# First units, a joint finish and gated linear attention on token partitions, in a two-layer hybrid encoder trunk

## What is computed

```
x += 0.5 * SwiGLU_1(RMSNorm(x))                 # 1024 -> 2816 -> 1024
proj = RMSNorm(x) @ w_in                        # q,k,v | q_g,k_g,v_g,gate,r_g
attn = rmsnorm(windowed attention with sinks and ALiBi)          # 512 wide
o    = gla_chunked(q_g, k_g, v_g, log_a)        # 4 heads x 128, chunks of 64
gla  = rmsnorm(o, per head) * silu(r_g)                          # 512 wide
x += concat(attn, gla) @ w_out
x += 0.5 * SwiGLU_2(RMSNorm(x))
```

## Time and profile before

| | |
|---|---|
| median of 3 runs | 932.29 us (932.19 to 932.37) |
| the profiled execution, its own time | 932.18 us |
| its span, first to last instruction | 930.6 us |
| PE busy | 920.4 us, 99% of the span, 8128 matmuls |
| weight loads of PE busy | 913.3 us, 98% |
| DVE, ACT, POOL busy | 606.8, 454.2, 2.8 us |
| loads | 169.04 MB, 182 GB/s over the span |
| granted PE clock, mean | 0.996 of full speed |

### The profile page before, as it was taken

How to read it: one execution, slowest core, us unless ns; L and a number is a source line. 1 busy time by engine, 2 the same in 40 slices (tenths; PEclk the granted TensorE clock), 3 DMA queues, 4 the chain that set the end, 5 groups by cost and what they waited for, 6 DMA issues and landing times.

```text
span 930.6 us, 19276 instructions
## 1 busy us (share of the span) xinstructions
PE 920.4 (99%) x8128; PEld 913.3 (98%) x8128; DVE 606.8 (65%) x699; ACT 454.2 (49%) x499; POOL 2.8 (0%) x6
## 2 busy tenths in 40 slices
PE   9999999999999999999999999999999999999996
PEld 9999999999999999999999999999999999999996
DVE  7765565687768665555685555567796785565554
ACT  6534434458646433444554344436675644434433
POOL 0000000000000000000000000000000000000001
PEclk9999999999999999999999999999999999999998
DMA  8765665563246665666556555655713675655631
GB/s 291 227 225 182 210 195 183 181 189 120 78 159 217 214 203 180 190 193 204 181 187 213 194 181 183 214 188 141 223 47 92 226 227 184 215 188 182 203 111 46
DMA packets 130996, 169.04 MB, mean 182 GB/s; under 512 B 3344, under 2 KB 116752, under 8 KB 130960
## 3 DMA queue, kind: packets, MB, share of 16 engines
q1 hardware_dynamic: 130384, 167.86, 56.5%
q10 hardware_dynamic: 576, 0.66, 0.2%
HBM read 167.46 MB, written 1.05 MB: 181 GB/s over the span
## 4 chain that ended last, share of the span: by engine, by line
PE 96%; DVE 1%; DMA 1%; issue 0%; ACT 0%; SPq 0%; POOLq 0%; DVEq 0%
PE ps L376 30%; PE ps L378 30%; PE ps L377 30%; PE ps L587 1%; PE ps L600 1%; DMA raw<-in_ffn_w_gate 1%; PE ps L437 0%; PE ps L724 0%; DVE wlo L1094 0%; PE ps L747 0%; PE ps L734 0%; SPq L260 0%; PE ps L429 0%; PE ps L794 0%; PE ps L682 0%
## 5 line engine op out<-in xcount | busy, mean ns | idle before, releaser
L1078 DVE TENSOR_TENSOR wlo<-raw,whi 128x2048 fp32r<-128x2048 f32 (+2 forms) x158 | 353.6, 2238 | 238.3 <-ACT whi L820 238.3
L376 PE MATMUL ps<-xhi,whi 128*128 128x256 f32 x1648 | 457.7, 278 | 0.0
L378 PE MATMUL ps<-xhi,wlo 128*128 128x256 f32 x1648 | 455.4, 276 | 0.0
L377 PE MATMUL ps<-xlo,whi 128*128 128x256 f32 x1648 | 455.4, 276 | 0.0
L820 ACT ACTIVATE whi<-raw 128x2048 fp32r<-128x2048 f32 (+2 forms) x158 | 295.8, 1873 | 146.4 <-PE ps L378 146.1
L376 PEld LDWEIGHTS ps<-xhi,whi 128*128 128x128 f32 x1648 | 309.5, 188 | 1.7 <-issue 1.0
L378 PEld LDWEIGHTS ps<-xhi,wlo 128*128 128x128 f32 x1648 | 309.6, 188 | 0.0
L377 PEld LDWEIGHTS ps<-xlo,whi 128*128 128x128 f32 x1648 | 309.5, 188 | 0.0
L376 PE MATMUL ps<-h_parts,whi 128*128 128x256 f32 x768 | 212.4, 277 | 0.9 <-DVE h_parts L1201 0.9
L377 PE MATMUL ps<-h_parts,whi 128*128 128x256 f32 x768 | 212.1, 276 | 0.0
L378 PE MATMUL ps<-h_parts,wlo 128*128 128x256 f32 x768 | 212.1, 276 | 0.0
(11 more groups left out here) (163 smaller groups left out, 498.2 us busy)
## 6 DMA issues: line engine op xcount, KB each, us to landing
raw<-in_ffn_w_down SPq DMA_DIRECT2D x44, 1024.0 KB, 4.9
raw<-in_ffn_w_gate SPq DMA_DIRECT2D x42, 1024.0 KB, 5.4
raw<-in_ffn_w_up SPq DMA_DIRECT2D x42, 1024.0 KB, 5.3
raw<-in_w_in SPq DMA_DIRECT2D x12, 1024.0 KB, 5.1
raw<-in_w_in SPq DMA_DIRECT2D x8, 512.0 KB, 4.6
raw<-in_w_out SPq DMA_DIRECT2D x8, 512.0 KB, 4.5
raw<-in_w_in SPq DMA_DIRECT2D x2, 1088.0 KB, 5.5
raw<-in_w_out SPq DMA_DIRECT2D x8, 256.0 KB, 3.7
```

What stands on the lines that cost most here:

```text
L376: pe.matmul(o, w_hi, x_hi, start=start, stop=False, skip_group_check=True)
L377: pe.matmul(o, w_hi, x_lo, start=False, stop=False, skip_group_check=True)
L378: return pe.matmul(o, w_lo, x_hi, start=False, stop=stop, skip_group_check=True)
L1078: nc.vector.tensor_tensor(lo, r, h.bitcast(F32), ALU.subtract).then_inc(lo_done, 1)
```

## The change

Five edits. (1) In the first units, `square_sums(0)` and `spread_r` move into the fifth piece, DVE's and ACT's pieces of the fourth unit move ahead and wait for less, and the low part of the first down unit is made in two halves. (2) The GLA products and both gate projections are computed with tokens on partitions; the sums of squares come from ACT's accumulator (`osum`), the gate is made by ACT directly from PSUM, norm and gate are applied by DVE in eight products of 128x128, and 8 transposes bring the result back; `gla_sums` and `o32` go. (3) ACT's table for Silu is called up after the attention's squares, not before the blocks. (4) The last two down units are finished together. (5) At the end fewer column sums, other places for the sums' additions, ten transposes that nobody reads (`KEEP`), and another order of two stores. Cut:

```diff
+            def finish_two(turn, grp):
+                def add(m, slot, ft, stop=False):
+                    w_hi, w_lo = weights(slot, ft, D, m * P, P)
+                    return three(sum_of(m, True), w_hi, w_lo, hhi[slot - 1][:, ft, :], hlo[slot - 1][:, ft, :], False, stop)
+                split_ready(1, turn)
+                for m in range(KT):
+                    add(m, 1, 0)
+                for ms in ((0, 1), (2, 3), (4, 5), (6,), (7,)):
+                    for m in ms:
+                        last = add(m, 1, 1)
+                    if ms[0] == 0:
+                        pe.wait_ge(hlo_done, grp + GROUPS)
+                        split_ready(2, turn)
...
+                    for m in ms:
+                        add(m, 2, 0)
+                        last = add(m, 2, 1, stop=True)
+                    last.then_inc(unit_done if ms[0] == KT - 1 else acc_pair, 1)
...
                     piece_lo(0, p, 2)
+                    if p == LAST:
+                        square_sums(0)
...
                     piece_lo(1, p, 7)
+                    if p == LAST:
+                        pe.wait_ge(s_cst, 16)
+                        spread_r(0, rs_y)
                     piece_lo(2, p, 0)
-                    if p == LAST - 1:
-                        square_sums(0)
-                pe.wait_ge(s_cst, 16)
-                spread_r(0, rs_y)
...
-                project(M_R0, t, tiles(0), attention_sums)
+                project_tokens(M_R0, t, [ps[0][:, 0:UC], ps[0][:, UC:2 * UC]], attention_sums)
...
+                for tt in range(TT):
+                    for h in range(GH):
+                        pe.matmul(o_tile(tt, h), AT[:, 4 * (h % 2) + 2 * (h // 2) + tt, :], vg[:, tt, h * P:(h + 1) * P],
+                                  start=tt == 0 and h < 2, stop=False, skip_group_check=True)
...
+                for c in range(1, NCH):
+                    for h in range(GH):
+                        j, b, r = h // 2, DK * (h % 2), CHUNK * (c % 2)
+                        last = pe.matmul(o_tile(c // 2, h)[r:r + CHUNK, :], qe[b:b + DK, j, c * CHUNK:(c + 1) * CHUNK],
+                                         Sta[b:b + DK, c - 1, j, :], start=False, stop=True, skip_group_check=True)
...
-                project(M_R1, t, tiles(0), gla_sums)
+                pe.wait_ge(sg_done, 4 * l + 2)
+                project_tokens(M_R1, t, [ps[0][:, 0:UC], ps[0][:, UC:2 * UC]])
...                                              # PE, behind M_WO + 1
-                        pe.wait_ge(o_ev, 2 * ev)
-                        spread([ps[1], ps[2]], 5 * l + 3, rs_y, 8).then_inc(rG_ps, 1)
+                        pe.wait_ge(og_done, 2 * ev)
+                        for h in range(GH):
+                            for tt in range(TT):
+                                last = pe.transpose(ps[3 * (h // 2)][:, (h % 2 * TT + tt) * P:(h % 2 * TT + tt + 1) * P],
+                                                    o_tok[:, tt, h * P:(h + 1) * P], ident)
...                                              # PE, end
-            tile_sums(4, first=True)
-            tile_sums(5)
-            tile_sums(6)
-            pe.wait_ge(sqsum_done, 3 * DEPTH + 2)
+            tile_sums(6, first=True)
+            pe.wait_ge(sqsum_done, 3 * DEPTH + 1)
             column_sums(sqsum[:, :])
             tile_sums(7, last=True).then_inc(ss_done, 1)
+            for _ in range(KEEP):
+                pe.transpose(ps[1][:, 0:P], ident, ident)
...                                              # ACT, mix
+                def gate_out(i):
+                    act.wait_ge(unit_done, ST + 3 * t + i + 1)
+                    c = UC * (i == M_R1)
+                    for tt in range(TT):
+                        nc.scalar.activation(sg_tok[:, tt, c:c + UC], ps[0][:, tt * UC:(tt + 1) * UC], ACT.Silu,
+                                             scale=rcol[:, tt:tt + 1]).then_inc(sg_done, 1)
+                gate_out(M_R0)
                 split_mix(10)
...
+                for p in range(2):
+                    act.wait_ge(o_ps, 2 * l + p + 1)
+                    for h in (p, p + 2):
+                        for tt in range(TT):
+                            e = nc.scalar.activation(o_sq[:, tt, h * P:(h + 1) * P], o_tile(tt, h), ACT.Square,
+                                                     accum_out=osum[:, GH * tt + h:GH * tt + h + 1])
+                    e.then_inc(osq_done, 1)
+                gate_out(M_R1)
                 split_mix(11)
...                                              # DVE, first block
+                    fourth_lo(0)
+                    norm_r(0, 0, rs_y)
+                    fourth_lo(1)
+                    norm_b(0)
+                    dve.wait_ge(rb_done, 1)
+                    gate_out(0, 0, 2)
+                    fourth_lo(2)
+                    up_out(0, 1, 7)
+                    fourth_lo(3)
+                    half_lo(0)
+                    h_lo(0, 0)
+                    half_lo(1)
...                                              # DVE, mix
+                dve.wait_ge(sg_done, 4 * ev)
+                for tt in range(TT):
+                    for h in range(GH):
+                        c = slice(h * P, (h + 1) * P)
+                        e = nc.vector.scalar_tensor_tensor(out=o_tok[:, tt, c], in0=o_tile(tt, h),
+                                                           scalar=rs_y[:, GH * tt + h:GH * tt + h + 1],
+                                                           in1=sg_tok[:, tt, c], op0=ALU.mult, op1=ALU.mult)
+                    e.then_inc(og_done, 1)
                 split_mix(11)
...                                              # POOL, DVE, end
+            add(flat(2, 4), flat(0, 2), flat(2, 4)).then_inc(pool_sum, 1)
+            pool.wait_ge(pool_sum, 1)
+            add(sqsum[:, :], sq[:, 2, :], sq[:, 3, :]).then_inc(pool_sum, 1)
...
+            last_residual(6, 7, 7)
+            dve.wait_ge(pool_sum, 2)
+            dve.wait_ge(sq_done, 2 * (3 * DEPTH - 1) + 3)
+            add_eps(sqsum[:, :], sqsum[:, :], sq[:, 4, :], D).then_inc(sum_step, 1)
+            dve.wait_ge(sum_step, 7 * (DEPTH - 1) + 9)
+            nc.vector.tensor_tensor(sqsum[:, :], sqsum[:, :], sq[:, 5, :], ALU.add).then_inc(sqsum_done, 1)
+            dve.wait_ge(unit_done, ST + 3 * DEPTH * TURNS)
+            last_residual(7, 8, 2)
```

More of the change, by code:

```diff
@@ L402, in up, with down @@
                 last.then_inc(unit_done, 1)
-            def down(slot, turn, hb, first, alone=False):
-                split_ready(slot, turn)
+            def down(slot, turn, hb, first, alone=False, halves=False):
+                if halves:
+                    pe.wait_ge(half_split, 1)
+                else:
+                    split_ready(slot, turn)
                 for ft in range(FT):
+                    if halves and ft:
+                        split_ready(slot, turn)
                     for m in range(KT):
@@ L544, in ffn @@
                 alone = f == 1 and l == DEPTH - 1
-                down(1, t + 1, 0, True, alone)
-                with pe.Fori(2, GROUPS) as g:
+                down(1, t + 1, 0, True, alone, l == 0 and f == 0)
+                with pe.Fori(2, GROUPS - alone) as g:
                     pe.wait_ge(a_done, grp + g)
@@ L740, in gla_sums @@
-                def gla_sums():
-                    pe.wait_ge(am_done, 4 * l + 2)
-                    for h in (0, 2, 1, 3):
-                        if h < 2:
-                            pe.wait_ge(osq_done, 2 * l + h + 1)
-                        for tt in range(TT):
-                            last = pe.matmul(ps[3][:, 2 * h + tt:2 * h + tt + 1],
-                                             sq[:, 4 + h, tt * P:(tt + 1) * P], ones[:, 0:1],
-                                             start=True, stop=True, skip_group_check=True)
-                    last.then_inc(oss_done, 1)
@@ L864, in ffn @@
                 grp = (2 * l + f) * GROUPS
-                if l or f:
-                    act.wait_ge(table_in, 2 * l + f)
-                    nc.scalar.activation(unread[:, :], ones[:, 0:2], ACT.Silu).then_inc(table_in, 1)
                 if l or f:
@@ L991, in mix @@
-                nc.scalar.activation(sg[:, 2:4, :], sg[:, 2:4, :], ACT.Silu).then_inc(sg_done, 1)
                 split_mix(12)
@@ L994, in mix @@
                 for b in range(2):
[L995 to L996 removed]
+                    act.wait_ge(og_ps, 2 * l + b + 1)
+                    nc.scalar.activation(xhi[:, 4 + 2 * b:6 + 2 * b, :], tiles(3 * b), ACT.Copy,
+                                         scale=par[:, G_GLA:G_GLA + 1]).then_inc(mhi_done, 1)
                 split_mix(14)
```

200 lines of the change are left out of this document (89 added, 111 removed).

## The result

The changed kernel takes 948.24 us (median of six runs, 947.81 to 954.5), the kernel before 932.33 beside it: ratio 1.016, 95% interval 1.0125 to 1.0195. Forecast was 925.6. The change makes the kernel 1.6% slower, though the waits for `sqsum` and `h_parts` that it was made to end are no longer in the list.

The account below looks back on a forecast made before the run. PE was taken to bound the kernel nearly throughout. Head -2.2, two mixers -3.2 and end -1.3 us gave -6.7 us on 932.18, so 925.5, median 925.6 us; range 923.8 to 928.0.

Parts of the forecast that it names:

- a slower pace of the 48-matmul units outside the places touched: Sign of being wrong: units away from the edits slow down; held for unchanged at 5.66 us a unit.
- E: Mixers: chain from M_R1 through second gate, eight products and low part becomes the longest; 934.4 us, chance 0.03.
- the price of the token form: Mixers: token-form units cost +0.19 us for a whole unit, taken as +0.1 each for M_R0 and M_R1.
- Head: First units: PE's early waits shrink and the first down unit starts at 29.5, not 31.75; -2.2 us.
- Mixers: Two mixers: column sums go, -1.7, token form +0.2, output units -0.1; -1.6 us each, -3.2 both.
- The state products: Mixers: 24 products at 55 to 68 ns, 1.3 to 1.6 us, no change; ends -0.45 and +1.1 us.
- Rival B: Mixers: the state products don't overlap, +1.1 us a mixer; 927.8 us, chance 0.10.
- C: Mixers: M_WO + 2 late from costlier products or squares, 0.5 to 1.2 us a mixer; 926.6 to 928.0, chance 0.09.
- End: Kernel's end: column sums -0.4, kept clock -0.5, store order -0.4; together -1.3 us, between -0.3 and -1.7.
- The sums: Kernel's end: 12 sum instructions instead of 20 let DVE go on sooner; -0.4 us, ends 0 and -0.7.
- rival D: Kernel's end: clock falls despite the ten transposes and ACT's order gives nothing; 926.5 us, chance 0.05.

Follow-up runs that it names:

- 12: Kernel before with five stands of PE, behind each mixer's eight spreads and behind the spread of blocks 2 to 4; 937.7 us, ratio 0.986.
- 9: Changed kernel with six stands of PE: ahead of block 1's first down unit, behind each mixer's transposes, behind blocks 2 to 4's spread; 928.2 us, ratio 0.979.
- 6: Changed kernel with a stand of PE behind the eight transposes of each mixer alone; 932.7 us, ratio 0.989.
- 1: Changed kernel with the GLA part, its gate, output norm and Silu table place as in the kernel before; 943.2 us, ratio 1.0025.
- 2: Kernel before with only the GLA part and the Silu table's place changed; 951.0 us, ratio 1.014.
- 17: Changed kernel as it is, run once more on another chip; 951.0 us, ratio 1.012.
- 5: Changed kernel with one stand of PE ahead of the first down unit of each feed-forward block; 929.9 us, ratio 0.989.
- 18: The kernel of 5, run once more on another chip; 930.9 us, ratio 0.992.
- 3: Changed kernel with eight more unread transposes of the old kind behind the eight of each mixer; 956.0 us, ratio 1.018.
- 4: Changed kernel with the 24 state products done a second time, unread, behind each mixer's transposes; 950.1 us, ratio 1.016.
- 13: Changed kernel with the weights of each three products in the order high, low, high; 948.3 us, ratio 1.017.
- 14: The kernel of 5 with its four stands lengthened to 0.65 us by a 192-column memset; 931.4 us, ratio 0.997.
- 11: The kernel of 5 with its four stands lengthened to 0.92 us by a 512-column memset; 951.2 us (recorded ratio covers two of twelve runs).

## Why the prediction was wrong

**The step that failed** is the ground of the sum: "a slower pace of the 48-matmul units outside the places touched, which I hold for unchanged". It changed in three blocks and the output units, +22.3 us, three times what the edit moved. I had read it in the rows, units behind column sums "already run at the slower pace in their second half", and priced it at 0.1 us for a unit. Since the pace holds through a whole block, and a block behind its spread is some 175 us long, the same 4.5 ns an instruction are 6.8 us there. No rival had this mechanism: E, the only slower one, priced a gate chain, and its wait didn't come. The rows also held both paces side by side, and I took them for a property of the form: of the two units in the earlier trace rows, M_KG starts three products in 340 ns and M_V0 in 353 (the trace, 225 and 231 us), and that is the whole of the 0.19 us that I called the price of the token form. M_V0 is slow in both mixers of all 20 traces; M_R1, in the same form, is fast in 17 of its 28 cases. Nor is 0.118 us "the pace of PE": it is 5.66 us over 48 with the gap in it, and the products step by 0.113.

**Head, -2.2 forecast, -1.6 measured.** Both waits go; the sums are at 20.51 (20.25 forecast). The down unit starts at 30.12 for 29.5, and the mis-sized term is the load: ACT waits for the down weights until 24.49, where I had 23.6 (issued 0.5 us later and landed after 5.6 us for 5.2). The chain behind it, to the end of `h_lo` at 30.06, took 5.6 us for 5.7. In the other traces with this head ACT starts on them at 24.0 to 25.3. And 0.2 us of the 1.6 is the pace of the fourth unit, not the edit.

**Mixers, -1.6 each forecast, -2.6 and -2.3 measured** up to the transposes. The state products were mis-sized: 43 ns, the lower bound, 0.47 us under before, where I took no change. The rest is pace: M_R1 ran fast where I added 0.1 us, and in the first mixer so did one unit ahead of the GLA part (0.2 us). Rival B is out, and C too: PE doesn't wait for the low part behind the transposes. The Trainium skill (TensorEngine Tiling (Array Packing), "When to Use Tiling"), which I did not follow, was nearer: it has such tiles gain up to twice the speed from the swap. The trace agrees in part: 1.49 to 1.02 us is a third less, not half.

**End, -1.3 forecast, -0.4 measured.** The sums gave -0.5 (-0.4 forecast), the kept clock -0.5 as forecast, so the clock did not fall, which was half of rival D; its other half, that ACT's order gives nothing, came. The stores, forecast -0.4, show +0.6 in this profile, but that is mostly the execution. From `rB` to the end the other new kernels' traces have 5.48 to 5.75 us and those with the old order 5.43 to 5.65, each set with SP's first store 0.3 to 0.5 us behind `rB`; where it is alike, the new order is within 0.1 us of the old. So it is the case with no gain, which was named, and without that one store the end would have given some -0.9 us, an estimate from these traces.

**The sum of the places touched**, -6.9 us, is near the -6.7 of the forecast by luck: the head and the end gave less, the mixers more, and part of it is pace. 12 less 9, -7.3 us, says about the same of two kernels at their best, and 6 at 926.46 comes near the 925.6. What the edit does at its places was right in the main, its price in the kernel was not. Two bounds of the forecast don't follow from their terms: no overlap gives -0.5 a mixer, not -0.4, and the end's terms span 0 to -1.6, not -0.3 to -1.7.

**Shown and open.** Shown: the kernel is slower because PE's pace is, +20.0 us in blocks 2 to 4 and +2.3 around them; this comes with the GLA part (1, 2, 17); it begins where M_WO follows M_R1; a stand or column sums can turn it (5, 6, 18); eight old transposes, small products or another order of the weights, put in at the places tried, don't bring the fast pace back (3, 4, 13). Open: what in PE holds the pace, why it turns at M_WO, and why six stands gave the fast one on one chip and the slow one on another. Length of stand, its place and the chip are not separated.

The Trainium skill (TensorE: Matmul & The Clock Gate, "Back-to-back issue gap") says that in a stream of weight loads and products the spacing is set by both, pipelined through a reorder window. The trace agrees in part: in the slow blocks one load in three is longer, 192 ns for 188, but in M_V0, slow as well, none is (188, 187 and 188). What the window holds no run here shows.

## What to carry to other kernels

When PE is the bound and never waits, count its matmuls in equal windows of the stretches that the edit does not touch, before and after: a few ns an instruction are worth more there than any wait. An edit that changes where PE's stream is interrupted, or the form of the units in it, may change the pace of all that follows, so price it with both paces, and look at several runs and chips before a difference of one or two per cent is given to the edit. Where a long even stretch is slow, try a stand of 0.4 to 0.65 us, from start to start, at its start: here it cost 0.3 to 0.5 and gave back up to 6.8, but not in every run, so check it on more than one chip.

## What the runs showed of the hardware that was not expected

- At a granted clock of 1.00 and with PE never idle, a load and a 256-column product have two spacings, 113.3 and 117.7 ns (340 and 353 ns for three), told in units with weights stationary by one weight load in three of 192 ns for 188. Which of the three it is holds through a stretch and differs between stretches.
- The pace holds unchanged for up to 180 us, and across many column sums and spreads. It turned at some of these, at waits, and with no interruption where a unit with weights stationary follows one with activations stationary: from fast to slow in 17 of 17 cases, from slow to fast in 5 of 11. One program's times so fall on levels some 6.8 us apart, a block each (932, 939, 946, 953).
- In the traces of 5, 14 and 18, seven stands of 0.38 us or 0.65 us found PE slow and six turned it to fast; three of 0.92 us on another chip (11) turned none. The same six stands left all blocks fast on one chip and slow on another.
- Ten unread transposes kept the clock at the 2.4 GHz level over a wait of 1.6 us, in which it had fallen before.
- 64x64 tiles with 128 moving columns that alternate between row halves take 43 ns each.
